# The low part of the weights by an adding DMA instead of a subtraction on GpSimd

## The reference, cut to what matters

```python
z = h @ w_in[l]                                   # 1024 x 7168
y_a = a @ w_conv_out[l]                           # 1024 x 1024
y_b = o @ w_attn_out[l]
x = x + (g_a * y_a + g_b * y_b) @ w_out[l]
u = causal_depthwise_conv(h @ w_up[l], ...)       # 1024 x 5632
x = x + (silu(u_gate) * u_val) @ w_down[l]        # 2816 x 1024
...
q, k, v, g, qi, wi, ki = split(x @ w_in)          # second block, two layers
y = (o * silu(g)) @ w_out
```

## Time and profile before

| | before |
|---|---|
| runs, us | 1734.93, 1735.26, 1730.39; median 1734.93 |
| profiled execution | span 1728.4 us from first to last instruction; no other time of it is given |
| what lies around the span | 6.5 us, if that execution took the median |
| TensorE (PE) busy | 1629.0 us, 94% |
| VectorE (DVE) busy | 1295.1 us, 75% |
| ScalarE (ACT) busy | 777.0 us, 45% |
| GpSimd (POOL) busy | 916.4 us, 53% |
| the core's 16 DMA engines | 25.7% of their time on the kernel's own queue, 144.34 MB |

### The profile page before, as it was taken

One profiled execution on the slowest core, in us unless ns is written; L12 is line 12 of the kernel. 1 busy time (PEld: TensorE's weight loads), 2 busy tenths in 40 slices (PEclk: granted clock), 3 DMA queues, 4 the chain that ended last, 5 costly groups with the idle time before them and its releaser, 6 DMA issues.

```text
span 1728.4 us, 22058 instructions
## 1 busy us (share of the span) xinstructions
PE 1629.0 (94%) x7740; PEld 1325.2 (77%) x7740; DVE 1295.1 (75%) x2088; ACT 777.0 (45%) x1381; POOL 916.4 (53%) x761
## 2 busy tenths in 40 slices
PE   7978689999999999999999999999999999999986
PEld 6766677878778888888888867777777887877766
DVE  6999998889865568718718478967776928788877
ACT  4111245656543344424424343367664325666642
POOL 3564454555526555545545543556657236666552
PEclk9999898999999999999999989999999999999998
DMA  5212132132232222222222331323223121211111
GB/s 184 82 62 73 49 98 86 56 98 86 67 123 88 97 96 98 98 97 95 96 95 90 113 97 66 117 78 90 83 84 110 64 67 56 70 59 58 60 37 49
DMA packets 49069, 145.74 MB, mean 84 GB/s; under 512 B 6784, under 2 KB 9344, under 8 KB 48960
## 3 DMA queue, kind: packets, MB, share of 16 engines
q1 hardware_dynamic: 48960, 144.34, 25.7%
HBM read 130.55 MB, written 2.10 MB: 77 GB/s over the span
## 4 chain that ended last, share of the span: by engine, by line
PE 73%; DVE 20%; ACT 3%; issue 2%; DMA 1%; POOL 1%; DVEq 0%; SPq 0%; POOLq 0%; ACTq 0%
PE bank L334 71%; DVE r L359 6%; DVE ext L359 5%; PE bank L340 2%; DVE ext L350 1%; DVE r L350 1%; DVE sp_lo L350 1%; DVE pt_lo L350 1%; ACT w_hi L344 1%; DMA k_both<-k_both 1%; DVE w_lo L350 0%; DVE q_both L359 0%; DMA w_raw<-in_weights 0%; DVE small L350 0%; DVE score L1739 0%
## 5 line engine op out<-in xcount | busy, mean ns | idle before, releaser
L365 POOL TENSOR_TENSOR w_lo<-w_raw,w_hi 128x512 fp32r<-128x512 f32 (+1 forms) x442 | 644.1, 1478 | 425.9 <-ACT w_hi L344 416.4
L334 PE MATMUL bank<-x_hi,w_hi 128*128 128x512 f32 x872 | 355.1, 407 | 13.1 <-ACT w_hi L344 7.2
L344 ACT ACTIVATE w_hi<-w_raw 128x1024 fp32r<-128x1024 f32 (+2 forms) x206 | 212.9, 1041 | 323.7 <-PE bank L334 318.9
L334 PE MATMUL bank<-x_hi,w_lo 128*128 128x512 f32 x872 | 347.1, 398 | 8.5 <-POOL w_lo L365 8.3
L334 PE MATMUL bank<-x_lo,w_hi 128*128 128x512 f32 x872 | 346.2, 397 | 0.0
L334 PEld LDWEIGHTS bank<-x_hi,w_hi 128*128 128x128 f32 x872 | 167.7, 192 | 49.5 <-ACT w_hi L344 14.1
L334 PEld LDWEIGHTS bank<-x_hi,w_lo 128*128 128x128 f32 x872 | 167.4, 192 | 46.9 <-POOL w_lo L365 10.2
L334 PEld LDWEIGHTS bank<-x_lo,w_hi 128*128 128x128 f32 x872 | 167.8, 192 | 31.4
L334 PE MATMUL bank<-w_lo,x_hi 128*128 128x256 f32 (+1 forms) x448 | 151.8, 339 | 15.0 <-POOL w_lo L365 15.0
L334 PE MATMUL bank<-a_hi,w_hi 128*128 128x512 f32 x416 | 162.0, 389 | 0.0
L334 PE MATMUL bank<-w_hi,x_hi 128*128 128x256 f32 (+1 forms) x448 | 157.0, 350 | 5.2 <-DMA k_both<-k_both 3.1
(11 more groups left out here) (210 smaller groups left out, 3307.2 us busy)
## 6 DMA issues: line engine op xcount, KB each, us to landing
w_raw<-in_weights SPq DMA_DIRECT2D x223, 512.0 KB, 3.6
k_both<-k_both SPq DMA_DIRECT2D x48, 128.0 KB, 2.3
turned<-raw SPq DMA_DIRECT2D x74, 64.0 KB, 2.0
alibi<-in_alibi SPq DMA_DIRECT2D x16, 256.0 KB, 2.9
w_raw<-in_weights SPq DMA_DIRECT2D x8, 384.0 KB, 3.0
r<-in_x SPq DMA_DIRECT2D x8, 256.0 KB, 6.8
r<-in_x SPq DMA_DIRECT2D x4, 512.0 KB, 7.4
out_y<-r SPq DMA_DIRECT2D x16, 128.0 KB, 1.8
```

Source lines behind the costliest of these rows:

```text
L334: return e.matmul(out, lhsT, rhs, start=start, stop=stop, skip_group_check=resumed)
L344: return self.act.run(lambda e: e.activation(out, in_, func, **kw), after, 0.07 + size(out) * 0.00086 + 0.09 * len(kw))
L365: return self.pool.run(lambda e: e.tensor_tensor(out, a, b, op), after, 0.06 + size(out) * 0.00225)
```

## The change

`w_lo` is no longer a subtraction. GpSimd writes minus `w_hi` into the `w_lo` buffer in one tensor_scalar over the whole chunk, and then issues a DMA that adds `w_raw` to it. The chunk counts as formed when that DMA has landed, for TensorE and for the next load into the raw buffer. The helper counts 1.0 us of GpSimd's time, 2.5 us of transfer and 2.0 us of landing for the planner. There is one semaphore a slot.

```diff
+    def add_by_dma(self, slot, out, in_, after):
+
+        if slot not in self.dma_sems:
+            self.dma_sems[slot] = [self.sem("dma_" + slot), 0]
+        entry = self.dma_sems[slot]
+        entry[1] += 16
+        self.pool.silent(lambda e: e.dma_start(out, in_, accum_op=ALU.add).then_inc(entry[0], 16), after, 1.0)
+        self.dma_time = max(self.dma_time, self.pool.time) + 2.5
+        return (entry[0], entry[1], self.dma_time + 2.0)
+
@@ split
         self.chunk_hi[c] = self.p_copy(hi, raw, after) if self.act_full else self.a_op(hi, raw, ACT.Copy, after)
         yield [self.chunk_hi[c]]
-        for n in range(2):
-            part = slice(w // 2 * n, w // 2 * (n + 1))
-            behind = self.pool.time > self.now + 1.0 and self.dve.time < self.now + 0.3
-            tok = (self.v_tt if behind else self.p_tt)(lo[:, part], raw[:, part], hi[:, part].bitcast(F32), ALU.subtract,
-                                                       after + [self.chunk_hi[c]])
-            if n == 0:
-                first = tok
-                yield [tok]
-        self.chunk_lo[c] = [first, tok]
+        minus = self.p_ts(lo, hi.bitcast(F32), -1.0, 0.0, ALU.mult, ALU.add, after + [self.chunk_hi[c]])
+        yield [minus]
+        self.chunk_lo[c] = [self.add_by_dma(f"add{s}", lo.bitcast(F32), raw, [minus])]
```

## The result

The changed kernel takes **1759.7 us** (median), the kernel before 1735.1 beside it: ratio 1.016, 95% interval 1.013 to 1.019. It is 1.6% slower. The forecast was 1731 us, no change; 1759.7 lies in its range (1708 to 1775), near the slow-landing rival's 1770. The span of the profiled execution is 1757.5 us.

A forecast was written before the change was run, and what follows sets the result against it. VectorE, slowed by GpSimd's subtractions, was taken to set the pace during the convolution, 45 to 227 us. Terms -22 + 20 + 3 - 8 + 3 = -4 us, with 6.5 us to the median, gave 1731 us; range 1708 to 1775.

The forecast's parts named there:

- slow-landing rival: Adding DMA lands in 7.2 us, so waits outweigh VectorE's gain (from 5.6 us upward): +35, 1770 us; chance 0.22.
- The subtractions go: Convolution window, 45 to 227 us: VectorE freed of GpSimd's subtractions, -22 us, bounds -27 and -11.
- The landing: Time from the adding DMA's issue to its landing: 5.1 us, low end 3.6, high end 7.4.
- x: Time from the issue of the adding DMA to its landing, taken as 5.1 us.
- four signs of being wrong: Landing over 5.6 us; issue over 2; k_both waits up over 12; negation costing VectorE as much as two subtractions.
- The steady tiles: Chunks wanted 9.85 us after GpSimd's start, new path 6.3 us: no cost unless the landing exceeds 8.7 us.
- The two-tile starts: Stage starts wanting the second chunk at once: new stalls, +20 us together, including 3 for the first chunk.
- The ten places: Chunks after 227 us wanted in less than 6.3 us (attn_out, out, up projection, w_down, qi): 17 us.
- Clock +3: Half clock behind four or five new stalls of about 2 us: +3 us, ends nothing and 14.
- VectorE elsewhere -8: Some twelve places outside the window where VectorE is on the chain beside GpSimd: -8 us, between -12 and 0.
- The queues +3, from 0 to +12: Copies to k_both delayed behind SyncE's waiting load and by DMA load rising to over half: +3 us.
- hold up the issue: Rival: VectorE delays GpSimd's DMA issue 2 to 3 us in the dense window, -11 for -22, 1742 us; chance 0.12.

The follow-up runs named there:

- the traffic run: Changed kernel, but the adding DMA adds the low tile onto the free raw tile and TensorE does not wait for it: 1725.9 us, ratio 0.997.
- held plain copy: Changed kernel, its DMA now a plain copy from the low tile that holds the raw tile, TensorE not waiting for it: 1711.7 us, ratio 0.988.

## Why the prediction was wrong

By its own steps, in their order:

- *The subtractions go*: **right**. -22 us, bounds -27 to -11; TensorE's lead at the end of the window is 17.1; from 45 us, where it lags 2.1 behind the first chunk's wait, it gains 19.2. The negation costs VectorE 0.8 for my 1.0. TensorE's idleness in the window is 23 us for my 15: six waits for landings, 11.8 us.
- *The landing*: x was taken as 5.1; alone it is 4.5 to 4.6, in the median of all 5.5. That is below the 5.6 from which the slow rival was to decide, yet the time came out as if above it. None of the four signs of being wrong that the prediction names appeared. The estimate by the Trainium skill ("DMA: Bandwidth & Descriptors", Anatomy of one DMA) was 4.4 with the bytes counted twice; counted once the same formula gives 3.2. With no other DMA under way the adding DMA took 4.5 to 4.6 and the plain copy 2.9. So the traces agree within 0.2 us for the adding DMA, and the estimate for the plain copy is 0.3 too high.
- *The steady tiles* cost nothing: **right**, and shown by a run of its own.
- *The two-tile starts*: **right in kind, and near in size by luck**. The ten places were put at 17 us, but the single prices in the prediction add up to 14.5, so its own sum is -6.5 and not -4. Their waits are 4.9 (attn_out), 2.7 and 1.9 (`out`), 1.3 and 1.4 (up projection), 0.6, 1.5 and 1.8 (end of w_down and what follows it), 1.5 and 2.5 (`qi`), together 20.1. For `out` the reading holds (2.7 with a landing of 6.6), for attn_out it doesn't (4.9 with one of 4.6, where 1.9 was said for 5.1). The first chunk: 2.9 for 3.
- *Clock +3*: **wrong**, by some 14 of the 33 us between forecast and result. From the end of the window to 1700 us the stretches at half the clock are 106.9 us long after and 58.0 before; TensorE is busy in 91.7 and 56.1 of them, so the clock cost 46 us for 28: **+18** (in the window and before it, -1). I counted only the four or five long waits at starts. Those in the heads were not counted, and neither was that a stretch at a wait of 4 to 5 us behind the window lasts 7 to 14 us, not the 6.8 of the one row that I had. Some stretches, of 6.8 us at 1447 and at 1628 us, have no such wait ahead of them.
- *VectorE elsewhere -8*: about right. Behind the window TensorE waits 23 us after and 34 before for anything but these DMAs, -11; part of that may be the order.
- *The queues +3, from 0 to +12*: **wrong**, 24 us without any wait of TensorE for `w_lo` (part of it through the clock: 7 us by 1700 us, 12 by 1501). I had reckoned with SyncE's waiting load and with a DMA share over half, and the bound came from copies alone. In my "2 x 1.2 us of all 16 engines" the doubled engine time is even there (measured: 38.0% of 1757.5 us over 231 DMAs, 2.9 us each), but it was used for the landing of the DMA itself and not for what it does to the others.
- In the **heads** I counted **no place at all**, as their chunks had slack to a path of 6.3 us, and this was **wrong**. Four waits for `w_lo` there and in the half-value tiles before the last heads (2.3, 1.6, 1.3 and 6.3 us) are 12 us, and the two for `k_both` that grew from 5.2 to 9.2 are 4 more. It is not x that failed for the four: the landings that ended them took 5.8, 4.5, 4.6 and 4.6 us, 4.9 in the mean for the forecast 5.1. The **issue** came late. Timelines of GpSimd and TensorE at the longest:

```profile
1389.80 1.04 POOL L388 TENSOR_SCALAR w_lo<-w_hi 128x1024 fp32r<-128x1024 f32 x1 [12.00 <-ACT w_hi L354]
1391.13 1.04 POOL L388 TENSOR_SCALAR w_lo<-w_hi 128x1024 fp32r<-128x1024 f32 x1 [0.29 <-ACT w_hi L354]
1392.12 1.77 POOL L338 DMA_DIRECT2D w_lo<-w_raw  x2
...
1396.78 0.80 PE L344 MATMUL bank<-w_lo,x_hi 128*128 128x512 f32 x1 [6.33 <-DMA w_lo<-w_raw]
```

The DMA of the first negation waits in GpSimd's queue until the second negation, which waits for ScalarE, is done. The prediction had said that nobody stands between a negation and its DMA, and put 0.1 us there. The median is 0.30, and for 69 of the 231 chunks it is over 0.5, as the planner lets another operation in. At the four it is 1.3 to 2.5 us, at attn_out and four of the other starts 0.8 to 1.0. Over the 14 chunks with the longer waits behind the window the issues are 11 us later than by 0.1 each; their landings take 5.2 us in the mean, as forecast. So from the start of the negation to the landing the four need 6.9 to 8.3 us for the forecast 6.3. A kernel in which the issue follows its negation at once was not run, so what that would bring is open. Landings of 7 to 10 us do occur, 42 of the 231, but only one of them (7.7, behind w_down) ended a wait of TensorE for `w_lo`.

The whole difference of the two spans, 29.1 us, adds up from the traces: -17.1 for the window, +32 of waits for `w_lo` behind it (20 at the starts, 12 elsewhere), +4 for `k_both`, -11 of other waits, +18 of half clock, and 3 that are left over, 2 of them behind 1700 us. Against the prediction's -4, the steps that failed are the clock at 3, the heads at nothing, and the queues, GpSimd's own above all, at next to nothing. (The 24 us of the traffic run are in these, in `k_both` and clock; they are not a term beside them.)

The rivals: the slow landing was nearest in time but not in its mechanism, since x stayed below its threshold; the loss came through clock, heads and neighbours. VectorE does not hold up the issue: GpSimd's 231 issues took 0.82 to 1.44 us. The Trainium skill ("SBUF — State Buffer", SBUF: two separate sides) says that GpSimd can't write the descriptors of its DMA while VectorE runs a two-port mode; the convolution's steps don't hold it up by these rows.

What stays open: how the 9 us of a held plain copy divide between SyncE's queue and the bytes; why the order of the change loses 6 to 10 us in the last heads in several kernels (half the clock costs 14 to 19 us there for 5 before, with no more idleness of TensorE); what sets off the half clock where no long wait stands ahead of it; and which stages GpSimd's negation slows behind the convolution.

## What to carry to other kernels

Cut a change by stage before costing it as a whole: this one was worth -1.4% in the one stage where VectorE sets the pace and +2.6% in all others, and a condition on the chunk's number keeps the first. If an engine is slowed by a neighbour at the SBUF, look for a third engine that isn't in the way: ScalarE's negation gave another 1.1%. And price a DMA by the time it takes of the DMA engines, for it makes its neighbours late as well, and look what the half clock added to TensorE's long waits: here 25 us more of waiting behind the window came with 18 us of clock. Where a queue runs in order, look also at what stands between an operation and the DMA that it sets free: here up to 2.5 us at chunks that TensorE waited for.

## What was not expected of the hardware

- An adding DMA within SBUF takes more than twice the DMA engines' time of a plain copy of the same size (38.7% against 17.8% of their span for 120 MB), and lands in 4.5 to 4.6 us alone for 2.9 (512 KB).
- ScalarE writing 1024 columns in 1.04 us leaves VectorE's steps at 0.66 us from start to start; GpSimd's tensor_scalar of the same shape adds 0.8 to one of them.
- GpSimd issues such a DMA in 0.88 us (median) in the middle of VectorE's convolution.
- SyncE's issues can take longer when GpSimd issues DMAs too: at 275.86 us, right behind two adding DMAs, four copies to `k_both` took 0.47 to 1.64 us each to issue, and the same four before 0.46 to 0.59. The mean of all 48 is 0.70 us after, 0.57 with plain copies within the SBUF and 0.50 with no DMA of GpSimd.
